# Block b's attention: six gate units inside the differential attention, another order in the merge, the first steps issued ahead

## The reference, cut to what matters

```
proj = u @ w_in
qa, ka, va, qd, kd, vd, ga, gd = jnp.split(proj, IN_SPLITS, axis=-1)
ya = stick_breaking_attention(heads(qa), heads(ka), heads(va))      # 8 heads of 64
yd = differential_attention(q1, q2, k1, k2, heads(vd), lam)         # 4 heads, values of 128
yd = rms_norm(yd, subln) * (1.0 - lambda_init)
merged = sigmoid(ga) * (ya @ w_branch_sb) + sigmoid(gd) * (yd @ w_branch_da)
return merged @ w_out
```

## Time and profile before

| what | us |
|---|---|
| median of 3 runs | 2776.15 |
| the profiled execution's own time | 2777.27 |
| its span, first to last instruction | 2776.0 |
| TensorE matmul busy | 2656.0 (96%) |
| VectorE, ScalarE, GpSimd busy | 900.2, 931.0, 1280.7 |
| mean granted TensorE clock | 0.976 of full speed |

### The profile page before, as it was taken

One profiled execution on the slowest core, in us unless ns is written; L12 is line 12 of the kernel. 1 busy time (PEld: TensorE's weight loads), 2 busy tenths in 40 slices (PEclk: granted clock), 3 DMA queues, 4 the chain that ended last, 5 costly groups with the idle time before them and its releaser, 6 DMA issues.

```text
span 2776.0 us, 30303 instructions
## 1 busy us (share of the span) xinstructions
PE 2656.0 (96%) x12126; PEld 2129.0 (77%) x12126; DVE 900.2 (32%) x1514; ACT 931.0 (34%) x1499; POOL 1280.7 (46%) x645
## 2 busy tenths in 40 slices
PE   8999999989999999999999999999977799899998
PEld 7888888866667888888887888877855588788886
DVE  3222111285664113444214554011056312311111
ACT  4223221235654223322223222223265423322221
POOL 4444444547774444444444444544433344444443
PEclk9999999999999999999999999988989899899999
DMA  4222222411002222455322554222200122122221
GB/s 158 99 99 92 92 99 87 130 61 46 1 1 69 98 92 103 151 186 190 106 96 105 183 182 160 92 79 76 99 14 1 37 93 98 54 99 92 94 97 59
DMA packets 87340, 261.51 MB, mean 94 GB/s; under 512 B 10528, under 2 KB 11808, under 8 KB 87200
## 3 DMA queue, kind: packets, MB, share of 16 engines
q1 hardware_dynamic: 83888, 255.46, 26.9%
q10 hardware_dynamic: 3312, 4.12, 0.5%
HBM read 257.44 MB, written 2.10 MB: 93 GB/s over the span
## 4 chain that ended last, share of the span: by engine, by line
PE 89%; DVE 4%; POOL 3%; ACT 1%; issue 1%; DMA 0%; DVEq 0%; ACTq 0%; SPq 0%; POOLq 0%
PE ps L282 79%; POOL prob L1724 3%; PE ps L293 1%; PE ps L1532 1%; PE ps L1851 1%; PE ps L1502 1%; PE ps L918 1%; PE ps L1000 1%; PE ps L1489 0%; PE ps L318 0%; PE ps L1816 0%; PE ps L1490 0%; PE ps L925 0%; POOL prob_d L2142 0%; PE ps L1840 0%
## 5 line engine op out<-in xcount | busy, mean ns | idle before, releaser
L269 POOL TENSOR_TENSOR split_ring<-raw_ring,split_ring 128x1024 fp32r<-128x1024 f32 x416 | 1018.1, 2450 | 1193.2 <-ACT split_ring L262 1193.2
L282 PE MATMUL ps<-hs,split_ring 128*128 128x512 f32 x6048 | 1395.5, 392 | 16.1 <-DVE hs L372 9.2
L282 PEld LDWEIGHTS ps<-hs,split_ring 128*128 128x128 f32 x6048 | 1140.8, 189 | 260.8 <-issue 12.4
L262 ACT ACTIVATE split_ring<-raw_ring 128x1024 fp32r<-128x1024 f32 x416 | 436.6, 1052 | 426.6 <-PE ps L282 414.3
L282 PE MATMUL ps<-ffn_act,split_ring 128*128 128x512 f32 x2112 | 495.4, 396 | 0.0
L282 PEld LDWEIGHTS ps<-ffn_act,split_ring 128*128 128x128 f32 x2112 | 397.8, 188 | 97.0
L568 ACT ACTIVATE ffn_act<-tmp 128x512 fp32r<-128x512 f32 x88 | 55.7, 632 | 395.9 <-DVE tmp L606 395.9
L1724 POOL TENSOR_SCALAR prob<-prob,small 128x512 f32<-128x512 f32 (+3 forms) x128 | 141.0, 1121 | 50.7 <-DVE small L1762 50.7
L606 DVE TENSOR_TENSOR tmp<-ps,tmp 128x512 f32<-128x512 f32 x44 | 30.4, 692 | 305.0 <-PE ps L282 305.0
L282 PE MATMUL ps<-split_ring,hs 128*128 128x512 f32 (+1 forms) x480 | 101.9, 373 | 0.0
L282 PEld LDWEIGHTS ps<-split_ring,hs 128*128 128x128 f32 x480 | 85.4, 188 | 15.9 <-issue 1.0
(11 more groups left out here) (333 smaller groups left out, 2592.3 us busy)
## 6 DMA issues: line engine op xcount, KB each, us to landing
raw_ring<-in_wstream SPq DMA_DIRECT2D x380, 512.0 KB, 3.4
ada_w<-in_w_ada SPq DMA_DIRECT2D x96, 256.0 KB, 3.6
raw_ring<-in_wstream SPq DMA_DIRECT2D x32, 384.0 KB, 3.0
sq<-in_w_ada SPq DMA_DIRECT2D x48, 256.0 KB, 3.6
x<-in_x_t SPq DMA_DIRECT2D x4, 512.0 KB, 6.5
decay<-in_decay ACTq DMA_DIRECT2D x8, 256.0 KB, 2.7
out_t<-x SPq DMA_DIRECT2D x8, 256.0 KB, 2.0
raw_ring<-in_wstream SPq DMA_DIRECT2D x4, 304.0 KB, 2.7
```

Of the source, the lines that this page charges most:

```text
L262: nc.scalar.activation(self.split[:, s, 0, :], self.raw[:, s, :], ACT.Copy).then_inc(self.sem("unit_hi"), 1)
L269: nc.gpsimd.tensor_tensor(self.split[:, s, 1, :], self.raw[:, s, :], self.split[:, s, 0, :].bitcast(F32), ALU.subtract).then_inc(self.sem( ...
L282: mm = self.nc.tensor.matmul(out, lhs, rhs, start=first and j == 0, stop=last and j == 2)
```

## The change

- Both `meet`s are gone, and so is `v_slot` with its copies: values are kept in `v_sb` and `v_d`, where the matmuls read them.
- Stick-breaking scores move to banks 4 to 6 (even m) and 0 to 2 (odd m), outputs to banks 7 and 3. Head 0's tables, q and k split, scores, softplus, sum and low part are issued within b.in.tm by every engine.
- The differential attention's scores use banks 4, 5, 6, 7, 0, turns banks 1 and 2, values bank 3. Its first four score banks are issued before the last sums of stick-breaking.
- Six gate units (`EARLY_GATES`, tiles 0 to 2 of the merge) become a stage `b.gates`, run in the turning banks: two before step 0, one within step 0, one at the head of each of steps 1 to 3. ScalarE copies them to `gate_b`; their sigmoids come at the merge's start.
- The splits of heads 1, 2 and 3 move within ScalarE's and VectorE's programs.
- The merge runs both gates of tile 3, then the joined units of tiles 0 to 3, then tiles 4 to 7 as before; branch banks alternate between (1, 2) and (6, 7), gates use 4 and 5. The shared merge functions are split in two; block a's is the same work as before.

The diff, cut to its core:

```diff
+EARLY_GATES = 6
+MERGE_B = [("gate", 3, 0), ("gate", 3, 1)] + [("both", _t, 0) for _t in range(4)]
+for _t in range(4, KD):
+    MERGE_B += [("gate", _t, 0), ("gate", _t, 1), ("both", _t, 0)]
...
-        ("b.merge", [UNIT] * 12, 2), ("b.out", [UNIT] * 4, 2),
+        ("b.gates", [UNIT] * EARLY_GATES, 1), ("b.merge", [UNIT] * len(MERGE_B), 1), ("b.out", [UNIT] * 4, 2),
...
# pe_tm_project
+            if (name, t, u) == ("b.in.tm", 1, 1):
+                self.pe_sb_scores(0)
...
+    SB_BANK = (4, 0)
+    SB_OUT_BANK = (7, 3)
...
# pe_stick_breaking; sb_scores(0) is no longer issued here
         for m in range(8):
             if m < 7:
-                scores(m + 1)
+                self.pe_sb_scores(m + 1)
             if m > 0:
                 times_v(m - 1)
+            if m == 7:
+                for i in range(4):
+                    self.pe_d_scores(0, i)
             sums(m)
         times_v(7)
...
+    def act_sb_ahead(self, t, u):
+        if (t, u) == (0, 0):
+            nc.scalar.wait_ge(sem("rstd_rows"), at("rstd_rows", "b.in"))
+            self.act_tables((self.prob_b[:, 0, 0:2 * P], "sb_sum"), (self.p2[:, 16, :], "distance"),
+                            (self.p2[:, 17, 0:6], "slopes"))
+        if (t, u) == (0, 1):
+            self.act_split_qk("s", 0, 4, 0, "summed")
+        if (t, u) == (0, 2):
+            nc.scalar.preload_act_table_set("natural_log_exp_and_others")
+            self.tables_here(nc.scalar, self.TABLES_SB)
...
+        if (t, u) == (1, 2):
+            self.act_softplus(0)
...
# act_stick_breaking
             probs(m)
+            if m == 0:
+                self.act_split(self.plan["b.gates"]["unit"] + LOOKAHEAD)
...
+    def dve_sb_ahead(self, t, u):
+        if (t, u) == (0, 2):
+            nc.vector.wait_ge(sem("k_lo_zero"), at("k_lo_zero"))
+            self.dve_sb_split(0)
+        if (t, u) == (1, 0):
+            self.dve_d_tables()
+        if (t, u) == (1, 3):
+            self.dve_sb_add(0)
...
     for _t in range(4):
-        D_TURN_USERS += [("t", _t, 0), ("t", _t, 1)] + ([("s", _t - 1)] if _t else []) + [("t", _t, 2)]
+        D_TURN_USERS += [("g", 0), ("g", 1), ("t", 0, 0), ("g", 2)] if _t == 0 else [("g", _t + 2), ("t", _t, 0)]
+        D_TURN_USERS += [("t", _t, 1)] + ([("s", _t - 1)] if _t else []) + [("t", _t, 2)]
...
+    def pe_d_gate(self, n):
+        g = self.plan["b.gates"]["unit"] + n
+        bank = self.pe_d_turn_bank("g", n)
+        if n < 2:
+            nc.tensor.wait_ge(sem("sb_prob"), self.at("sb_prob", 7, 2))
+        nc.tensor.wait_ge(sem("unit_lo"), g + 1)
+        for j in range(KD):
+            mm = self.three_passes(bank, slice(j * P, (j + 1) * P), self.hs[:, 0, j, :], self.hs[:, 1, j, :], g % RING,
+                                   j == 0, j == KD - 1)
+        mm.then_inc(sem("unit_used"), 1)
+
+    def act_d_gate(self, n):
+        nc.scalar.wait_ge(sem("unit_used"), self.plan["b.gates"]["unit"] + n + 1)
+        nc.scalar.activation(self.gate_b[n], self.d_turn_bank("g", n), ACT.Copy).then_inc(
+            sem("gate_kept"), to("gate_kept", n))
...
# pe_differential
-        for i in range(5):
-            self.pe_d_scores(0, i)
+        self.pe_d_scores(0, 4)
+        self.pe_d_gate(0)
+        self.pe_d_gate(1)
         for t in range(4):
+            if t > 0:
+                self.pe_d_gate(t + 2)
             for i in range(2):
                 self.pe_d_turn(t, i)
+                if t == 0 and i == 0:
+                    self.pe_d_gate(2)
                 if t < 3:
                     self.pe_d_scores(t + 1, i)
...
# act_differential
+        self.act_d_exps(0, range(5))
         self.act_split_qk_d(1)
-        self.act_d_exps(0, range(5))
+        self.act_d_gate(0)
+        self.act_split(gates + 1)
         for t in range(4):
+            if t == 0:
+                self.act_d_gate(1)
+                self.act_split(gates + 2)
             if t > 0:
                 self.act_d_square(t - 1)
+            if t > 0:
+                self.act_d_gate(t + 2)
+            if 0 < t < 3:
+                self.act_split(gates + t + 3)
             self.act_d_turned(t, 0)
+            if t == 0:
+                self.act_split_qk_d(2)
+                self.act_d_gate(2)
+                self.act_split(gates + 3)
+            if t == 1:
+                self.act_split_qk_d(3)
...
-            if t < 2:
-                self.act_split_qk_d(t + 2)
...
# pool_differential: pool_split(gates + 1) and (gates + 2) before step 0, then at the end of each step
+                self.pool_split(gates + t + 3)
...
# dve_differential
         self.dve_d_maxima(0, 1)
+        self.dve_sb_keep(3)
         self.dve_d_maxima(0, 2)
-        self.dve_split_qk_d(1)
...
             self.dve_d_mix(0, part)
+        self.dve_split_qk_d(1)
         for t in range(4):
+            if t == 1:
+                self.dve_split_qk_d(3)
+                self.dve_d_slope(3)
             self.dve_d_turned(t)
...
-            if t < 2:
-                self.dve_split_qk_d(t + 2)
-                slope(t + 2)
+            if t == 0:
+                self.dve_split_qk_d(2)
+                self.dve_d_slope(2)
...
# pe_merge_b
+                if tile == 3:
+                    nc.tensor.wait_ge(sem("da_exp"), at("da_exp", 3, z))
                 else:
+                    nc.tensor.wait_ge(sem("sigmoid"), at("sigmoid", "b", tile - 1, z))
...
+                if tile == 0:
+                    nc.tensor.wait_ge(sem("da_lo"), at("da_lo", 3))
+                if tile > 1:
+                    nc.tensor.wait_ge(sem("branch"), at("branch", "b", tile - 2, z))
...
# tensor
-        self.meet(nc.tensor)
         self.pe_stick_breaking()
-        self.meet(nc.tensor)
...
# gpsimd
+        for t, u, g in self.units("b.in.tm"):
+            if (t, u) == (1, 1):
+                self.pool_sb_lo(0)
+            self.pool_split(g + LOOKAHEAD)
+        for m in range(1, 8):
+            self.pool_sb_lo(m)
+            if m == 1:
+                self.pool_split(g + LOOKAHEAD + 1)
```

More of the change, by code:

```diff
@@ L2291, in pe_merge @@
[L2291 removed]
+    def pe_merge(self):
         nc, sem, to, at = self.nc, self.sem, self.to, self.at
[L2293 to L2296 removed]
+        parts = ((self.att_hi, self.att_lo), (self.ret_hi, self.ret_lo))
+        for tile, part, g in self.units("a.merge"):
             nc.tensor.wait_ge(sem("unit_lo"), g + 1)
+            if tile == 0:
+                nc.tensor.wait_ge(sem("gr_scaled"), at("gr_scaled", 4 + part))
+            elif part < 2:
+                nc.tensor.wait_ge(sem("merge_scaled"), at("merge_scaled", tile - 1, part))
+            else:
+                nc.tensor.wait_ge(sem("branch"), at("branch", "a", tile - 1, part - 2))
+            if tile == 0 and part > 1:
+                nc.tensor.wait_ge(sem("part_lo"), at("part_lo", ("att", "ret")[part - 2], 7))
+            self.pe_fm_tile(g, part, self.h_parts if part < 2 else parts[part - 2]).then_inc(sem("unit_used"), 1)
@@ new lines, in act_merge @@
+    def act_merge(self):
+        nc, sem, to, at = self.nc, self.sem, self.to, self.at
+        nc.scalar.preload_act_table(ACT.Sigmoid)
+        for tile, part, g in self.units("a.merge"):
+            self.act_split(g + LOOKAHEAD)
+            if part < 2:
+                nc.scalar.wait_ge(sem("merge_scaled"), at("merge_scaled", tile, part))
+                nc.scalar.activation(self.tmp[:, part, :], self.tmp[:, part, :], ACT.Sigmoid).then_inc(
+                    sem("sigmoid"), to("sigmoid", "a", tile, part))
+            if part == 3:
+                self.act_mix_hi("a", tile)
+        nc.scalar.preload_act_table(ACT.Sqrt)
@@ new lines, in pe_merge_b @@
+    def pe_merge_b(self):
+        nc, sem, to, at = self.nc, self.sem, self.to, self.at
+        for (kind, tile, z), (t, u, g) in zip(MERGE_B, self.units("b.merge")):
+            nc.tensor.wait_ge(sem("unit_lo"), g + 1)
+            if kind == "gate":
+                if tile == 3:
+                    nc.tensor.wait_ge(sem("da_exp"), at("da_exp", 3, z))
+                else:
+                    nc.tensor.wait_ge(sem("sigmoid"), at("sigmoid", "b", tile - 1, z))
+                self.pe_fm_tile(g, self.B_GATE_BANKS[z], self.h_parts).then_inc(sem("unit_used"), 1)
@@ new lines, in act_merge_b @@
+        for (kind, tile, z), (t, u, g) in zip(MERGE_B, self.units("b.merge")):
+            self.act_split(g + LOOKAHEAD)
+            if kind == "gate":
+                nc.scalar.wait_ge(sem("unit_used"), g + 1)
+                if tile > 3:
+                    nc.scalar.wait_ge(sem("mixed"), at("mixed", "b", tile - 1))
+                nc.scalar.activation(self.tmp[:, z, :], self.ps[:, self.B_GATE_BANKS[z], :], ACT.Sigmoid).then_inc(
+                    sem("sigmoid"), to("sigmoid", "b", tile, z))
+            else:
+                self.act_mix_hi("b", tile)
@@ L2352, in dve_merge, with dve_merge_b @@
+        nc.scalar.preload_act_table(ACT.Sqrt)
+    def dve_merge_b(self):
+        nc, sem = self.nc, self.sem
```

(13 more changed lines are left out.)

421 lines of the change are left out of this document (202 added, 219 removed).

## The result

The changed kernel took **2730.53 us** (median of 4 runs, 2729.52 to 2732.4), the kernel before on the same chip 2776.28 (4 runs). The ratio is 0.983, 95% interval 0.982 to 0.985; the forecast was 2732. Its profiled execution took 2729.52 (span 2728.2) against 2777.27 before: 47.75 us less in the two profiled executions, 45.75 less by the medians.

What follows compares the result with a forecast made beforehand. The prediction took TensorE to bound the kernel, its time won where it idles or runs slow. Terms summing to 43.8 us, taken as 44 off the 2776.15 us median, gave 2732 us, range 2727 to 2738 (58%).

Steps and rivals of the forecast that it cites:

- start, to scores(3): Stick-breaking's start: head 0's work under the projection brings scores(2) 18.8 us earlier, less 1.6 for clock; net 17.2 us.
- seam, with two gates: Stick-breaking to differential attention: score banks cover a 1.67 us wait, two gates fit before the first turn; 10.9 us won.
- step 0: First differential attention step: grows 4.2 us while taking in a gate of 5.45; 1.3 us won.
- step 1: Second attention step: new 5.1 us wait for VectorE's turned copy, 1.6 for clock; 21.5 against 17.1, 1.1 us won.
- step 2: Third attention step: no split left, 9.1 us waits for slope and k gone; 15.7 against 18.1, 7.9 us won.
- step 3: Last attention step: gate hides most mix waits; 14.3 against 15.8 us, 6.9 us won.
- merge: Final stage, eighteen units left: its first unit loses its slow start, no new wait; 0.5 us won.
- VectorE beside GpSimd: Attention steps: five GpSimd ring splits among the mixes slow VectorE; 2 us charged, bounds 0 and 12.
- The clock's charge: At scores(2): a 3.5 us TensorE idle may lower the granted clock; 1.6 us charged, bounds 0 and 2.
- the early start fails: Rival, in the projection: queued tables or head 0's split delay its units or scores(0); loses up to 18.8 us, 2751; 4%.
- the slower rival: Hole at scores(2) drops the clock and the stick-breaking loop stays at 1.2 GHz; +56 us, 2788; 3%.
- the rival: Locked ports, attention steps: five ring splits each delay a mix or split on the path, 12 us instead of 2; 2742; 8%.

Runs made afterwards that it cites:

- head3_split: Changed kernel with head 3's q and k split ahead of ScalarE's gate 3 copy and behind VectorE's turned copy and first maximum; 2727.12 us.
- splits_first: Changed kernel with GpSimd's ring split in each of steps 0 to 2 moved ahead of that step's scalings; 2730.43 us.
- combined: Changed kernel with three edits: pair 1's split early, GpSimd's ring splits ahead of its scalings, head 3's split behind VectorE's turned copy; 2720.69 us.
- changed_again: The changed kernel itself measured once more, nothing altered, for scatter; 2730.71 us.
- pair1_early: Changed kernel with ScalarE's split of pair 1's q and k issued in the projection's last unit, ahead of softplus(1); 2727.97 us.
- start_late: Changed kernel with head 0's work issued after the projection again, barriers still out and table transfers still early; 2744.02 us.
- dscores_late: Changed kernel with the first four differential score banks issued after stick-breaking's last values instead of before its last sums; 2735.05 us.

## Why the prediction was right

The time was 2730.53 for 2732, inside the forecast's own range, by the mechanism it named: idle stretches of TensorE filled with six gate units and an early head 0. The stretches of the two profiled executions, cut at the same instructions, against the forecast's terms:

| term | forecast | measured | from |
|---|---|---|---|
| start, to scores(3) | 17.2 | 17.9 | 2057.66 - 2039.74 |
| seam, with two gates | 10.9 | 11.3 | 24.65 for 25.0 from head 6's values to the first turn, + 10.9 |
| step 0 | 1.3 | 1.4 | 14.0 long, forecast 14.1 |
| step 1 | 1.1 | 1.5 | 21.05, forecast 21.5 |
| step 2 | 7.9 | 8.1 | 15.5, forecast 15.7 |
| step 3 | 6.9 | 7.5 | 13.8, forecast 14.3 |
| merge | 0.5 | 0.0 | 99.8, forecast 99.3 |
| VectorE beside GpSimd | -2 | not apart | lies in the steps |
| sum | 43.8 | 47.7 | 45.75 by the medians |

The total is closer than its terms. The stretches sum to 3.9 us more than the forecast; half of that is the 2 us charged for VectorE beside GpSimd, most of which was not there, and 2.0 us are scatter of the profiled pair (below). That the medians came within 2 us of 43.8 is in part luck.

- **Start.** scores(2) came 19.5 us earlier (forecast 18.8), idle before scores(1) 0.69 (0.7), the hole before scores(2) 3.15 (3.5). The clock's charge, 1.6, was right: the round took 10.87 us at 0.84, and 9.33 once the hole was gone. The undo took back 12.3 us of the 17.7 that the trace shows from the projection's end to scores(3). The other 5.4 stay with what the undo left alone, the early transfers and the removed barriers (the idle before scores(0) was 7.7 us for 11.8); which of the two it is was not tested. The rival "the early start fails" falls.
- **Loop and seam.** The rounds from scores(3) on stayed at 9.6 us in the mean (2039.74 to 2078.08 is four), at 1.00 of the clock, so the slower rival had its trigger (a hole of over 3 us) but not its effect: the clock was back within the round (the same matmul of 128x512 took 0.63 us at 2029.17 and 0.40 at 2034.88). Two gates stand ahead of the first turn with no idle, and undoing the cover of the 1.67 us wait brought it back.
- **Step 1.** The new wait was the right one, on VectorE's turned copy behind head 3's split, 4.08 us for 5.1; `head3_split` removed it alone. Of the missing 1.0, about half is that TensorE itself came later (its matmuls between gate and turn wait 0.67 for slope, held by GpSimd), and the rest that both engines' chains were a little shorter: ScalarE's from gate copy to the end of the split 5.8 us (2131.98 to 2137.74) for 6.1, VectorE's behind it 2.4 for 2.6.
- **Steps 2 and 3.** Within 0.2 and 0.6 us; the old waits for slope, 9.1 us in two, are 0.67 in one.
- **VectorE beside GpSimd** was mis-sized on both sides. The hold is longer than the 0.6 us of the earlier trace rows: 2.0 on a slope, 2.1 on three mixes. The forecast had judged that row by its length and called it undecided; the end of its neighbour, 0.28 us before its own, was in the same trace. The splits also fell in part elsewhere: step 0's on the slope, not on a mix, those of steps 1 and 2 each on three mixes. The price on the path is 0.1 us by `splits_first`, for behind each held instruction stood another wait that was as late, and some 1.3 once one of those was gone (`combined`). The forecast took 2 and the rival 12.
- **Idle of before.** The forecast called all four steps half idle. Step 0 was busy for 9.48 of 9.90 us; its term, 1.3, was worked out from its own rows and does not rest on this.
- **The waits** came to 18.3 us where the cross-check had some 20: 37.0 fewer than before, for its 35.5.

The profiled pair differs by 47.75 us and the medians by 45.75: the profiled run before lay 1.0 above its median and the one after 1.0 below, so 2.0 us is scatter of the pair. Shown by undoing are the gates' place (22.2 us by the totals), the early issue (12.3) and the seam's cover (1.7). The other 10 us or so of the 45.75 (barriers and early transfers, moved splits, the merge's order) were not undone one by one. Open is what makes the granted clock differ behind equal waits.

## What to carry to other kernels

Where a stage of dependent steps leaves the matrix engine half idle beside a stage that is solid and independent of it, count the idle of the first by its waits and move whole units of the second into it: here six units of 5.45 us took 22.2 us off, a third of it in matmuls that ran at a higher clock (7.9 of the 23.7 us of the stretch). Then read, per engine, what is queued ahead of the instruction that ends each new wait; moving one split behind a copy was worth 4.7 us in its step. A neighbour that slows an instruction is worth removing only if nothing else is as late: here it won 0.1 us alone. And compare edits worth under 5 us by a stretch within each trace, cut at the same instructions, since the work ahead of it moved by 6.5 us between traces.

## What was not expected of the hardware

- A split of GpSimd from SBUF to SBUF held VectorE's slope, mixes and remainders of k, all on SBUF, to its end: 0.29 us became 2.30, 1.42 became 3.54, and in the changed kernel two remainders of k took 3.49 us (at 2109.36) where two others took 1.39. A reduction from PSUM beside such a split kept its 1.22 us. The hold shows as a long instruction, not as a wait.
- The granted clock at the same place, after the same waits, came out either way. After waits of 0.25, 0.85 and 0.94 us (each to 0.04) values(3) took 2.42 us in the changed kernel, `changed_again` and `pair1_early`, 4.09 and 4.11 in `start_late` and `head3_split`, and 3.49 in `dscores_late`; after waits of 0.25 and 1.9 us it took 2.42 in `combined` and 4.11 in `splits_first`. It moves a total by 1.7 to 2.9 us, as much as half of the edits tried here, and upstream of block b's attention it made 4.9 us between two traces. What decides it is open.
